# The down product of an MLP by Strassen's scheme over two pairs, with x kept in DRAM and added to by DMA

## What is computed

```python
def layer_output(...):
    ...
    h = x + merged @ p["w_out"]
    f = jnp.square(jax.nn.relu(rmsnorm(h, p["norm_mlp_g"]) @ p["w_up"])) @ p["w_down"]
    return h + f
```

## Time and profile before

| | |
|---|---|
| median of 3 runs | 2558.39 us (2558.21 to 2558.9) |
| profiled execution, its time | 2558.83 us |
| its span, first to last instruction | 2557.0 us |
| TensorE (PE) busy | 2539.2 us, 99% |
| VectorE (DVE) busy | 1698.8 us, 66% |
| ScalarE (ACT) busy | 1025.9 us, 40% |
| GpSimd (POOL) busy | 393.2 us, 15% |
| DMA | 175.33 MB, mean 69 GB/s |

### The profile page before, as it was taken

The page is one execution under the profiler, slowest core; times in us unless marked ns, Lnnn a source line. Parts: engine busy times, 40 slices in busy tenths (PEclk is TensorE's granted clock), DMA queues, the critical chain, the costliest instruction groups (busy, mean ns, idle before and its releaser), DMA issues.

```text
span 2557.0 us, 43498 instructions
## 1 busy us (share of the span) xinstructions
PE 2539.2 (99%) x18096; PEld 2454.6 (96%) x18096; DVE 1698.8 (66%) x2436; ACT 1025.9 (40%) x1777; POOL 393.2 (15%) x328
## 2 busy tenths in 40 slices
PE   9999999999999999999999999999999999999998
PEld 9999877999999999999999998779999999999997
DVE  8679766598555565656675797665975656565556
ACT  5464355445232322323424644553443323232325
POOL 0123244100000000000001233541000000000002
PEclk9999999999999999999999999999999999999999
DMA  4112201212232322323221121012132323232322
GB/s 157 50 64 65 59 11 45 91 58 67 63 83 63 79 70 65 79 63 87 93 85 58 58 70 51 11 45 95 55 73 72 74 67 79 63 87 63 83 63 81
DMA packets 71984, 175.33 MB, mean 69 GB/s; under 512 B 11200, under 2 KB 14368, under 8 KB 71792
## 3 DMA queue, kind: packets, MB, share of 16 engines
q1 hardware_dynamic: 49600, 129.62, 15.6%
q0 software_dynamic: 22048, 42.91, 9.2%
q10 hardware_dynamic: 144, 0.04, 0.0%
HBM read 158.83 MB, written 11.36 MB: 67 GB/s over the span
## 4 chain that ended last, share of the span: by engine, by line
PE 95%; DVE 3%; issue 1%; ACT 0%; DMA 0%; SPq 0%; POOL 0%; DVEq 0%; POOLq 0%; ACTq 0%
PE ps L1120 29%; PE ps L760 26%; PE ps L1091 24%; PE ps L969 5%; PE ps L984 4%; PE ps L1039 2%; PE ps L916 2%; PE ps L827 1%; PE ps L941 1%; DVE mxp L2014 0%; PE ps L1117 0%; PE ps L789 0%; DVE xall L2273 0%; PE ps L848 0%; DVE msq L2381 0%
## 5 line engine op out<-in xcount | busy, mean ns | idle before, releaser
L2296 DVE TENSOR_TENSOR xall<-xall,ps 128x536 f32<-128x536 f32 (+1 forms) x504 | 356.8, 708 | 246.6 <-PE ps L1120 241.1
L1120 PE MATMUL ps<-fh,whi 128*128 128x268 f32 (+1 forms) x2016 | 412.4, 286 | 0.0
L1120 PE MATMUL ps<-fh,wlo 128*128 128x268 f32 (+1 forms) x2016 | 412.4, 286 | 0.0
L1120 PE MATMUL ps<-fl,whi 128*128 128x268 f32 (+1 forms) x2016 | 412.2, 286 | 0.0
L1499 ACT ACTIVATE whi<-raw 128x512 fp32r<-128x512 f32 x218 | 136.4, 628 | 644.5 <-PE ps L1120 490.2
L2566 POOL DMA_DIRECT2D raw<-in_wst x120 | 105.5, 879 | 1373.5 <-DVE wlo L2148 794.3
L1120 PEld LDWEIGHTS ps<-fh,whi 128*128 128x128 f32 x2016 | 314.7, 189 | 0.3 <-issue 0.2
L1120 PEld LDWEIGHTS ps<-fl,whi 128*128 128x128 f32 x2016 | 314.1, 189 | 0.0
L1120 PEld LDWEIGHTS ps<-fh,wlo 128*128 128x128 f32 x2016 | 314.0, 189 | 0.0
L2148 DVE TENSOR_TENSOR wlo<-raw,whi 128x512 fp32r<-128x512 f32 x218 | 150.4, 692 | 215.5 <-ACT whi L1499 214.3
L2014 DVE TENSOR_REDUCE mxp<-ps 64x1 f32<-64x64 f32 (+11 forms) x384 | 140.5, 372 | 56.0 <-PE ps L916 49.3
(11 more groups left out here) (558 smaller groups left out, 5815.2 us busy)
## 6 DMA issues: line engine op xcount, KB each, us to landing
raw<-in_wst SPq DMA_DIRECT2D x140, 512.0 KB, 3.7
draw<-in_wst SPq DMA_DIRECT2D x128, 256.0 KB, 2.9
raw<-in_wst POOLq DMA_DIRECT2D x120, 256.0 KB, 4.0
xall<-in_xT SPq DMA_DIRECT2D x16, 537.0 KB, 7.1
x_scratch<-xall POOLq DMA_DIRECT2D x8, 537.0 KB, 3.9
xall<-x_scratch SPq DMA_DIRECT2D x8, 537.0 KB, 4.9
rc<-sum_scratch POOLq DMA_DIRECT2D x16, 268.0 KB, 4.1
ra<-qr SPq DMA_DIRECT2D x16, 134.2 KB, 2.4
```

The lines of the kernel that those rows point to most:

```text
L1120: mm = nc.tensor.matmul(ps[:, 2 * s + q, 0:HN], wt, rhs[:, q * HN:(q + 1) * HN], start=(kk == 0 and i == 0), stop=(kk == 1 and i == 2))
L2296: V.tensor_tensor(xq, xq, pair_slot(DOWN_SLOT[n % 3], L), ALU.add).then_inc(S["d_add"], 1)
```

## The change

**What it does.** Pairs 1 to 14 are taken two by two, in seven groups g of a layer (q = 0, 1 within one). The down product of a group is Strassen's scheme too, over (two row tiles of x) x (two halves of the tokens), with the sum over the group's four blocks of D_FF inside. For each of the four pairs of row tiles i there are seven products P1 to P7 of 12 matmuls. The left operands are sums of weight blocks, made by VectorE (`block_sum`, 13 per group, 256 columns) and for i = 0 partly by three DMAs (`down_sum`); the right operands are the four results f of each q and three combinations (t1, t2, t3, t4 from `combine`), so that seven high and seven low parts are made per q.

Products accumulate in PSUM in chains: P6 is added to P1, then P7, then P4 in one bank pair, P3 to P5 in another, P2 in a third. x is no longer in SBUF during the groups (its place holds the new operands): pair 0 writes x to DRAM, eight times 537 KB per layer. Each group makes 16 results of 128x536: ScalarE copies a stage of the chain into one of **five staging tiles** (`part_out`), VectorE adds the partner to it (`part_add`, not for P4), and POOL issues an accumulating DMA of it into x in DRAM (`add_part`). A staging tile is used again when its DMA has landed. Before the closing pair SP reads x back. The scratch for the DMA descriptors of POOL's queue is set to 4096 bytes.

Weights come in 30 fills per group: 0 to 13 for the up products, then four for each i: (P5, P1), (P6, P2), (P7, P3), (P4). The core of the diff:

```diff
+DOWN_FILL = [("P5", "P1"), ("P6", "P2"), ("P7", "P3"), ("P4",)]
+CHAIN_SLOT = [0, 3, 0, 3, 0, 3]
+X_COPY = {"P1": (0, 0, 0), "P5": (1, 1, 1), "P6": (2, 0, 1), "P4": (3, 1, 0)}
+X_ADD = ["P3", "P7", "P2"], ["P2", "P7", "P3"]
+N_STAGE = 5
...
 # TensorE, waits of a down product (i = 0..3)
+                        elif name == "P6":
+                            at("x_copy", 4 * i + 1)
+                        elif name == "P7":
+                            at("x_copy", 4 * i + 3)
...
+                            if i == 0:
+                                at("f_hi", 7 * q + F_NAMES.index(f) + 1)
+                            for k, (a, c) in enumerate((("h", "h"), ("l", "h"), ("h", "l"))):
+                                if i == 0 and c == "l":
+                                    at("f_lo", 7 * q + F_NAMES.index(f) + 1)
+                                for t in range(2):
+                                    mm = nc.tensor.matmul(ps[:, 2 * slot_ + t, 0:HN], ring(u, whi if a == "h" else wlo)[:, wc],
+                                                          fop[q, f + c][:, t * HN:(t + 1) * HN],
...
 # TensorE, wait of t4n
+                        else:
+                            at("c_add", 3 * q + 3)
...
 # ScalarE
+                    def part_out(i, name):
+                        n, row, _ = X_COPY[name]
+                        at("prod", down_at(i, name) + 1)
+                        before, count = staged_before(L, g, i, n)
+                        if count:
+                            act.wait_ge(S[before], count)
+                        nc.scalar.activation(quarters(stage_of(L, g, i, n)[:, 0:N2]), src, ACT.Copy, scale=-1.0 if row else 1.0).then_inc(S["x_copy"], 1)
...
 # ScalarE, around the start of i = 1
+                    part_out(0, "P4")
+                    fill(19)
+                    fill(20)
+                    part_out(1, "P1")
...
 # VectorE, middle of the up products of q = 0 and 1
+                    fill(8)
+                    combine(0, "t1")
+                    c_add(0, 2)
...
 # VectorE, end of a group
+                    part_add(3, "P2")
+                    next_fill(0)
+                    part_add(3, "P7")
+                    part_add(3, "P3")
+                    next_fill(1)
...
 # POOL
+                def add_part(g, i, name):
+                    pool.dma_start(x_scr[2 * i + row, :, a:b], stage_of(L, g, i, n)[:, 0:b - a], accum_op=ALU.add).then_inc(S[done], 16)
+
+                def opening():
+                    for m in range(8):
+                        w("d_add", DOWN.index((m, 0)) + 1)
+                        save_x(m)
+                        if m == 3:
+                            up_sum(0, 0, 0)
+                    up_sum(0, 0, 3)
+                    up_sum(0, 0, 1)
+                    w("x_out", 128)
...
 # SP, before the closing pair
+                    w("prod", PER["prod"])
+                    quarter(NPAIR - 1, 0)
+                    quarter(NPAIR - 1, 1)
+                    for m in range(8):
+                        for n in (1, 3) if m % 2 else (0, 2):
+                            name, count = staged_before(L, NGROUP - 1, m // 2, n)
+                            sp.wait_ge(S[name], count + 16)
+                        sp.dma_start(x[m], x_scr[m]).then_inc(S[f"x_in{m}"], 16)
```

More of the change, by code:

```diff
@@ new lines, in group, with used @@
+                def group(g):
+                    def used(k):
+                        w("u_lo", groups("u_lo", g) + k + 1)
+                    used(up_fill(0, "b21"))
+                    up_quarter(g, 1, "a11")
+                    used(up_fill(0, "b22"))
+                    up_quarter(g, 1, "a21")
+                    used(up_fill(0, "t3n"))
+                    up_quarter(g, 1, "a12")
+                    used(up_fill(0, "t4n"))
+                    up_quarter(g, 1, "a22")
+                    used(up_fill(1, "b21"))
+                    down_half(g, 0, 1)
+                    used(up_fill(1, "b22"))
+                    down_half(g, 0, 0)
+                    used(up_fill(1, "t3n"))
+                    down_half(g, 1, 0)
+                    used(up_fill(1, "t4n"))
+                    down_half(g, 1, 1)
+                    for i in (0, 1):
+                        used(down_fill(i, 2))
+                        down_half(g, i + 2, 0)
+                        used(down_fill(i, 3))
+                        down_half(g, i + 2, 1)
+                    used(down_fill(2, 2))
+                    up_quarter(g + 1, 0, "a21")
+                    used(down_fill(2, 3))
+                    up_quarter(g + 1, 0, "a11")
+                    used(down_fill(3, 2))
+                    up_quarter(g + 1, 0, "a12")
+                    used(down_fill(3, 3))
+                    up_quarter(g + 1, 0, "a22")
@@ L709, in _ @@
+                opening()
+                for n_group in range(NGROUP):
+                    group(n_group)
+                closing()
             n_store = 0
@@ L1129, in _ @@
+                plain_pair(0)
+                for n_group in range(NGROUP):
+                    group(n_group)
+                plain_pair(NPAIR - 1)
         @block.scalar
@@ L1497, in up_hi @@
                     else:
[L1498 removed]
+                        w("prod", PER["prod"] - GROUP["prod"] + FILL_DONE[26 + u])
                     nc.scalar.activation(ring(pairs("u_hi", j) + u, whi), src, ACT.Copy).then_inc(S["u_hi"], 1)
@@ L2408, in _, with d_sum @@
-                mlp()
+                def d_sum(at, j, n):
+                    opening, closing = j == 0, j == NPAIR - 1
+                    m, h = (DOWN if not closing else LAST_DOWN if L == DEPTH - 1 else CLOSE_DOWN)[n]
+                    at("down", n + 1)
+                    if n == 0 and opening:
+                        w("res_add", 8)
+                    if closing:
+                        w(f"x_in{m}", 48)
+                    if n >= 8 and closing and L == DEPTH - 1:
+                        a, b = END_AT[n // 8]
+                        xq = x[m][:, a:b]
+                        V.tensor_tensor(xq, xq, ps[:, 2 * DOWN_SLOT[n % 3], 0:b - a], ALU.add).then_inc(S["d_add"], 1)
+                        return
+                    xq = quarters(x_half(m, h))
+                    V.tensor_tensor(xq, xq, pair_slot(DOWN_SLOT[n % 3], L), ALU.add).then_inc(S["d_add"], 1)
@@ new lines, in fill_lo @@
+                def fill_lo(g, k):
+                    dve.wait_ge(S["u_hi"], L * PER["u_hi"] + groups("u_hi", g) + k + 1)
+                    spot = groups("u_hi", g) + k
+                    i, name = FILLS[k]
+                    if i < 2:
+                        quarter_ = UP_QUARTER[i][{"b11": "a11", "t3n": "a11", "b21": "a12", "t4n": "a22"}.get(name, "a21")]
+                        src, hi, dst = raw_all[:, 512 * quarter_:512 * quarter_ + 512], ring(spot, whi), ring(spot, wlo)
+                    else:
+                        n = DOWN_FILL.index(name)
+                        src = down_source(i - 2, n)
+                        hi, dst = (ring(spot, t).rearrange("p (b n) -> p b n", b=2)[:, 0:1 if n == 3 else 2, :] for t in (whi, wlo))
+                    V.tensor_tensor(dst, src, hi.bitcast(F32), ALU.subtract).then_inc(S["u_lo"], 1)
@@ L2573, in _ @@
+                opening()
+                for n_group in range(NGROUP):
+                    group(n_group)
+                up_sum(NGROUP, 0, 2)
                 if L < DEPTH - 1:
```

1070 lines of the change are left out of this document (774 added, 296 removed).

## The result

| | before | changed |
|---|---|---|
| median (4 runs each) | 2558.3 us (2558.19 to 2558.9) | 2717.98 us (2708.14 to 2720.27) |
| profiled execution, its span | 2557.0 us | 2716.3 us |
| mean granted clock of TensorE | 0.998 | 0.977 |

A forecast was written before the change was run, and what follows sets the result against it. TensorE, busy 99% without gaps, was taken as the bound. From 2558.8 us, 82.8 of matmuls went off and 106 (groups), 12 (opening pair) and 8 (closing pair) came on: 2602 us, slower by 1.7%, range 2540 to 2640.

The forecast's parts named there:

- that rival: x's accumulates into DRAM land late, at 8 us each: 6 us of waits per group, 2686 us; chance 0.1.
- The first rival: ScalarE and VectorE hand over faster, so the queue-order waits don't come: 2518 us, half of it 2555; chance of faster 0.28.
- 1, P6: Pair q = 1: P6 waits for t2's low part, with fill 15's late weights: 3.3 us per group.
- 2, P7 and P2: P7 waits 1.6 us per group for ScalarE's copy of P6, P2 0.3 for b21's low part.
- 3, P6 of i = 1: Adding P6 waits for ScalarE's copy of P1, queued behind fill 20: 0.8 us per group.
- 4, t2 of q = 0: At a group's start t2 waits for its weights, summed by DMA: 0.3 us per group.
- 4, t4n of q = 0: t4n waits for t3n's c_add, behind fill 8 and a chain of DMA sums: 1.3 us per group.
- POOL to ScalarE reading what has landed 3.96: Time in us from POOL's issue of a weight-block sum to ScalarE reading it, taken from the earlier profile.
- term 4: Weight-block sums by DMA at a group's start delay t2 by 0.3 us and t4n by 1.3 per group.
- The new accumulates into DRAM cost TensorE nothing: 16 accumulates of x per group, 268 KB, land in 4.1 us (bounds 3.2 and 8), with no wait for TensorE.
- Term 6, the closing pair: b22's late sum costs 2.75 us, sharing with x's reads 1.25; twice, +8 us.
- Term 5, the opening pair: Weight-block sums behind x's saves on POOL cost 3.6 us there and 2.4 at group 0's t2; twice, +12 us.

The follow-up runs named there:

- The last version: Changed kernel with reordered queues, x's last accumulates behind the next group's down sums, P1's copy (i = 1) before fill 20, low b21 before P7's part_add: 2552.52 us.

## Why the prediction was wrong, point by point

**Right.** 672 matmuls fewer, -82.8 us. The sign, and the kind of the cause: queue order at P6, P7, P6 of i = 1 and t4n. No rival took its place: x's accumulates landed at 5.6 us, over the 5.1 that I called free, but ScalarE waited for staging tiles 24.5 us in 21 times, never over 2.3, not the 6 us a group of that rival. (The first rival's "half of it gives 2555" should read 2560 by its own terms: half of 84 us on top of 2518. Nothing hangs on it.) The walk's sizes, over 14 groups:

| step | forecast | measured waits |
|---|---|---|
| 1, P6 | 46 | 28.7 (27.2 + 1.5), and P6's weights in part of 5.0 |
| 2, P7 and P2 | 27 | 8.2 and 2.3 |
| 3, P6 of i = 1 | 11 | 12.1 (a few at other products) |
| 4, t2 of q = 0 | 4 | 23.0 |
| 4, t4n of q = 0 | 18 | 15.5 |
| not forecast: b22 of q = 0, t4n of q = 1, P1 | 0 | 10.1 + 12.8 + 5.2, and the rest of 5.0 |
| all | 106 | 123 |

P7's 1.6 us stood only where P6's wait was short (775.14, 1.41 us); else P6's wait covered it. Counting both in full was too much by some 30 us, and it hid part of what was too little elsewhere: that the two sums come out near each other, 106 and 123, is in part luck. Groups of 97.4 us in layer 0 stand against the 90.8 that were to show the steps right.

**Wrong, in order of size.** The forecast had 126 us (106 + 12 + 8) to set against the 242 measured. The difference of 116 is 37 us of waits, up to 57 of clock and an estimated 20 of restarts. So two steps failed: every wait was priced at its own length, and the new DMAs were taken to cost the others nothing.
1. **The clock had no term.** Every wait was priced at its own length. The groups and the two ends together lost up to 57 us to 1.2 GHz, and another 20 to 0.15 us at each restart. The run with low t2 first shows the clock almost alone: 1 us less of waits there, 20 us less time.
2. **The step "POOL to ScalarE reading what has landed 3.96"** in term 4. It is the price of a sum with nothing beside it. In a group's first 20 us the sums took 5.3, 5.9 and 4.8. With x's accumulates shrunk to a row, 45 us go (waits of t2, b22 and P1, and of the closing pair, follow it). "The new accumulates into DRAM cost TensorE nothing" was the sentence that failed: I asked only whether staging tiles come free in time, not what the transfers do to others.
3. **Term 6, the closing pair**, +8 for +28.5. "1.25 for the sharing" took the reads' effect as a quarter of one tile. The two sums landed 8.1 and 9.2 us after their issue at 1300.38 and 1310.19, beside the eight reads and, at first, three accumulates of x, with the DMA engines' share at 1.00 and 1.06. The page of the Trainium skill "DMA: Bandwidth & Descriptors", section "Issuing engines are not separate DMA queues", said that all issuers share the 16 engines. The trace now agrees, with these numbers.
4. **Term 5, the opening pair**, +12. Measured 15.5, and 4.7 us before t2 of the first group where 2.4 was meant, and the half clock: undoing POOL's order was worth 35 us.
5. **Terms by queue order left out:** fill 14, which waits for a sum by DMA (issued at 1046.89, read at 1051.24), stood ahead of b11's square on ScalarE and of c_add on VectorE. I followed fill 15 and 16 and not 14; P1 and t4n of q = 1 paid 18 to 23 us.

The page of the Trainium skill "DMA: Bandwidth & Descriptors", section "Anatomy of one DMA — SWDGE (gpsimd) path", gives 2.0 us plus bytes over 436 GB/s, as an estimate 2.6 us for 268 KB. The plain write at 3.1 comes near it, the accumulate of the same bytes at 5.6 does not.

**What stays open.** Whether more or fewer than five staging tiles change anything, and the size of the descriptor scratch, were not tried. The last version still has 57 us of waits in its listing, at the weights of P1, P6 and P3 above all, where the sums for the down product end; no run took these away. How much clock a given set of waits costs was seen to change from kernel to kernel (14 to 29 us between P1 and P7 for the same waits); no run shows what decides it.

## What to carry to other kernels

When a kernel is bound by one engine without a gap, a change that saves 3% of its work can only win if every hand-over still keeps its lead: walk each queue around each DMA wait, first of all those that stand ahead of cheap instructions on which others depend. Price a new wait with what follows it (slow clock, restart), and price a new stream of DMAs by the transfers that it runs beside, not by its own landing. The same work, put in other places of five queues, moved this kernel from 2718 to 2553 us.
